# First modulation by column quarters beside the first four GLU units, later modulation in half-height blocks

## What is computed

```python
def modulation(c, w_ada, b_ada):
    m = jax.nn.silu(c) @ w_ada + b_ada              # 9 conditioning vectors; w_ada is 2048 x 12288
    return jnp.split(m[:, None, :], 6, axis=-1)

sh1, sc1, g1, sh2, sc2, g2 = modulation(c, w_ada, b_ada)
h = rmsnorm(x, norm1_g) * (1 + sc1) + sh1
z = h @ w_in                                        # 2048 x 5120
za, zg, q, k, v = jnp.split(z, ...)
u = za * jax.nn.sigmoid(zg)                         # the GLU, 1024 channels
```

## Time and profile before

| | us |
|---|---|
| runs | 3962.62, 3974.74, 3953.63 |
| span of the profiled execution (its own time is not listed apart from these) | 3945.3 |
| TensorE busy | 3630.9 |
| VectorE busy | 2664.1 |
| ScalarE busy | 446.6 |
| GpSimd busy | 1088.6 |

### The profile page before, as it was taken

One profiled execution on the slowest core, in us unless ns is written; L12 is line 12 of the kernel. 1 busy time (PEld: TensorE's weight loads), 2 busy tenths in 40 slices (PEclk: granted clock), 3 DMA queues, 4 the chain that ended last, 5 costly groups with the idle time before them and its releaser, 6 DMA issues.

```text
span 3945.3 us, 34389 instructions
## 1 busy us (share of the span) xinstructions
PE 3630.9 (92%) x12423; PEld 1928.8 (49%) x12423; DVE 2664.1 (68%) x4415; ACT 446.6 (11%) x975; POOL 1088.6 (28%) x865
## 2 busy tenths in 40 slices
PE   4899998997996799789989999999989899999997
PEld 1566544466552574356833444444455344444443
DVE  1258852148888885878976766677688765555666
ACT  2100004110000350011700000000043000000000
POOL 1000001106434543444153222222234422222331
PEclk8999999998998779899999999999999999999998
DMA  9878763459999998999699999999978999999997
GB/s 364 278 233 265 246 214 124 150 195 393 410 413 417 370 379 326 396 386 398 228 415 421 421 414 418 421 418 416 421 285 337 420 420 396 421 422 421 422 418 311
DMA packets 348738, 1402.89 MB, mean 356 GB/s; under 512 B 25601, under 2 KB 150489, under 8 KB 207606
## 3 DMA queue, kind: packets, MB, share of 16 engines
q0 software_dynamic: 117056, 832.57, 52.4%
q1 hardware_dynamic: 230512, 563.29, 38.1%
q10 hardware_dynamic: 1008, 4.98, 0.3%
HBM read 1375.24 MB, written 31.55 MB: 357 GB/s over the span
## 4 chain that ended last, share of the span: by engine, by line
DMA 48%; PE 27%; issue 14%; DVE 8%; POOL 3%; ACT 0%; SPq 0%; DVEq 0%; POOLq 0%; ACTq 0%
DMA R<-in_u_experts,MS 34%; DMA R<-in_v_experts,MS 10%; PE bank L868 8%; PE bank L896 7%; PE bank L1083 4%; DMA R<-in_w_ada 3%; POOL R L749 3%; DVE R L2242 2%; PE bank L808 1%; DVE R L2127 1%; DVE R L2034 1%; PE bank L785 1%; PE bank L1090 1%; DMA R<-h_scratch 1%; PE bank L1145 1%
## 5 line engine op out<-in xcount | busy, mean ns | idle before, releaser
L749 POOL DMA_INDIRECT R<-in_u_experts,MS x640 | 899.9, 1406 | 1639.2 <-DVE MS L2127 1354.6
L2127 DVE CUSTOM_DVE_ANT_0 R<-R 128x2048 f32<-128x2048 f32 x374 | 857.2, 2292 | 412.0 <-DMA R<-in_u_experts,MS 390.7
L1290 PE MATMUL bank<-R,RB 128*128 128x512 f32 x2304 | 1019.4, 600 | 46.9 <-DMA R<-in_v_experts 46.7
L1290 PE MATMUL bank<-RB 128*128 128x512 f32 x1792 | 778.2, 592 | 0.0
L1290 PEld LDWEIGHTS bank<-R,RB 128*128 128x128 f32 x2304 | 440.7, 192 | 615.5 <-issue 552.9
L2127 DVE CUSTOM_DVE_ANT_0 R<-R,RB 128x2048 f32<-128x2048 f32 x266 | 608.5, 2288 | 107.1 <-DMA R<-in_u_experts,MS 105.7
L1290 PEld LDWEIGHTS bank<-RB 128*128 128x128 f32 x1792 | 340.5, 190 | 428.6 <-issue 428.6
L2242 DVE SCALAR_TENSOR_TENSOR R<-R,MS 128x2048 f32<-128x2048 f32 x128 | 301.4, 2355 | 197.3 <-DMA R<-in_v_experts,MS 196.9
L868 PE MATMUL bank<-RB,R 128*128 128x256 f32 (+1 forms) x1536 | 400.4, 422 | 27.6 <-DMA R<-in_w_pq 24.4
L868 PEld LDWEIGHTS bank<-RB,R 128*128 128x128 f32 x1536 | 294.5, 193 | 126.4 <-DMA R<-in_w_pq 25.0
L1083 PE MATMUL bank<-RB,R 128*128 128x384 f32 x1024 | 333.3, 486 | 1.4 <-ACT RB L1450 0.7
(11 more groups left out here) (353 smaller groups left out, 2214.4 us busy)
## 6 DMA issues: line engine op xcount, KB each, us to landing
R<-in_v_experts SPq DMA_DIRECT2D x144, 1024.0 KB, 9.1
RB<-in_v_experts SPq DMA_DIRECT2D x112, 1024.0 KB, 9.3
R<-in_w_ada SPq DMA_DIRECT2D x48, 2048.0 KB, 13.2
R<-in_w_in SPq DMA_DIRECT2D x20, 2048.0 KB, 18.0
R<-in_w_in SPq DMA_DIRECT2D x24, 1024.0 KB, 28.4
R<-in_w_out SPq DMA_DIRECT2D x8, 2048.0 KB, 8.2
R<-in_w_pq SPq DMA_DIRECT2D x8, 2048.0 KB, 10.1
R<-in_w_out SPq DMA_DIRECT2D x16, 1024.0 KB, 15.9
```

Of the source, the lines that this page charges most:

```text
L749: pool.indirect_dma_start(dst, None, table, bass.IndirectOffsetOnAxis(ap=expert[T_ % 2][:, c:c + 1], axis=0)).then_inc(signal, 16)
L1290: x = pe.matmul(PB[4 * h + q][:, :], W[:, i, h * P:(h + 1) * P], vring[slot][:, q * PW:(q + 1) * PW], start=(i == 0), stop=(i == NKEY - 1))
L2127: V.tensor_tensor_reduce(u, u, x, 1.0, 0.0, ALU.mult, ALU.add, dots[t % 2][:, h * TOPK + s:h * TOPK + s + 1]).then_inc(dots_done, 1)
```

## The change

**First modulation in quarters.** The 4096 columns are cut into 32 pieces of 4 k by 512 columns, 1 MB each (`ada_piece`, four slots, in the place of ring slots 2 and 3). Order: column quarter q (0 to 3), in it scale, then shift, in it four groups of k. In a sum, the four k of a piece go to the four strips of rows (`ada_sums`), so that four pieces give 128 rows with the partial sums of 4 x 4 k. ACT copies them out (`keep_sums`), and `turn_mods` multiplies them with a 0/1 matrix (`group_sum`) onto the turned bias: this adds the four strips and turns them at once. Quarter q gives scale and shift for k = 4q to 4q+3. Sums of quarter 0 stand ahead of the projection (pieces 0 to 3 ahead of the transposes of x, 4 to 7 behind them and the conv cache), those of quarters 1 to 3 between the matmuls of the first four GLU units, which now run side by side over k in banks 0 to 5 (`first_unit`). With k = 12 to 15 the four units are finished one after another.

**Later modulation in halves.** 16 blocks of 512 columns, each in two halves of 8 k (`wide` slots 2 and 3, `modulate_half`, `load_ada_half`), 3, 3, 2 halves ahead of units 5, 6, 7 and so on (twelve units). None stands beside the first four units. DVE adds 16 blocks of 512 columns; its order of sums, convolutions and gates is written out.

**Start.** SP issues x first, then pieces 0 to 3, both w_in slots, and the other pieces. POOL makes its constants ahead of its loads, and issues the conv cache without a wait. DVE computes the distance rows first, ACT stores them. Two of the five squares of x move from ACT to DVE.

The core of the diff (semaphore counts that only follow are left out):

```diff
-            for n in range(NM1):
-                chunk, i = (1, n) if n < 8 else (0, n - 8)
...
+            for t in range(T):
+                sp.dma_start(xt[t], xp[t] if t < TP else xs).then_inc(s_x, 16)
+
+            def load_ada_piece(n):
+                q, shift, j = n // 8, n // 4 % 2, n % 4
+                if n >= 4:
+                    sp.wait_ge(mod_done, n - 3)
+                at = (0 if shift else D) + q * PW
+                sp.dma_start(ada_piece[:, j], wv["w_ada"][:, 4 * j:4 * j + 4, at:at + PW]).then_inc(s_bx[j], 16)
+
+            def load_ada_half(m):
+                c, half = divmod(m, 2)
+                sp.wait_ge(mod_done, ADA - 2 + 2 * m if m < 2 else ADA + m - 1)
+                sp.dma_start(wide[:, 2 + half], wv["w_ada"][:, 8 * half:8 * half + 8, 2 * D + c * PW:2 * D + (c + 1) * PW]
+                             ).then_inc(w_in_s[2 + half], 16)
+
+            for n in range(4):
+                load_ada_piece(n)
+            for b in range(2):
+                load("w_in", b, b * CC)
+            for n in range(4, ADA):
+                load_ada_piece(n)
+            for m in range(2):
+                load_ada_half(m)
+            for b in range(2):
+                sp.wait_ge(z_done, 2 * b + 2)
+                load("w_in", b, BW + b * CC)
+
+            m = 2
+            for u in range(12):
+                for _ in range(HALVES[u % 3]):
+                    if m < 2 * NMC:
+                        load_ada_half(m)
+                    m += 1
+                i, b, c = 1 + u // 4, u // 2 % 2, u % 2
+                if c == 1 and i < 3:
+                    sp.wait_ge(z_done, 4 + u + 1)
+                    load("w_in", b, (i + 1) * BW + b * CC)
...
+            def ada_sums(n):
+                q, shift, j = n // 8, n // 4 % 2, n % 4
...
+                for i in range(4):
+                    m = pe.matmul(PB[6 + shift][32 * i:32 * i + 32, :], cT32[:, 4 * j + i, :], ada_piece[:, j, i, :],
+                                  start=(j == 0), stop=(j == 3))
+                m.then_inc(mod_done, 1)
+
+            def turn_mods(q):
+                pe.wait_ge(s_mc, 2 * q + 2)
+                for shift in range(2):
+                    for i in range(4):
+                        at = (0 if shift else D) + (4 * q + i) * P
+                        out = PB[7][:, 64 * shift + 16 * i:64 * shift + 16 * i + NCND]
+                        pe.matmul(out, mrow[:, at:at + P], ident[32:32 + NCND, 32:32 + NCND],
+                                  start=True, stop=False)
+                        m = pe.matmul(out, mod_sums[shift][:, i * P:(i + 1) * P], group_sum, start=False, stop=True)
+                m.then_inc(s_modT, 1)
+
+            def modulate_half(m):
+                c, half = divmod(m, 2)
+                bank = PB[4 + (c + 2) % 4]
+                if half == 0 and c >= 4:
+                    pe.wait_ge(mod_free, c - 3)
+                elif half == 0 and c >= 2:
+                    pe.wait_ge(z_free, 3 + c)
+                pe.wait_ge(w_in_s[2 + half], 16 * (c + 1))
+                for k in range(8):
...
+                mm.then_inc(mod_done, 1)
...
+            for n in range(4):
+                ada_sums(n)
+            turn_x(0, KT + 4)
+            turn_conv_cache()
+            for n in range(4, 8):
+                ada_sums(n)
+            pe.wait_ge(s_bada, 32)
+            turn_mods(0)
             pe.wait_ge(cc_E, 4)
-            def glu_and_modulation(i, first):
...
+            for q in range(3):
+                n = 8 * (q + 1)
+                for i in range(4):
+                    for u in range(4):
+                        first_unit(u, 4 * q + i)
+                        if 4 * i + u in (0, 1, 3, 4, 6, 7, 9, 10):
+                            ada_sums(n)
+                            n += 1
+                        elif 4 * i + u == 12:
+                            turn_mods(q + 1)
+            for u in range(4):
+                for k in range(12, KT):
+                    first_unit(u, k)
+
+            m = 0
+            for u in range(12):
+                for _ in range(HALVES[u % 3]):
+                    modulate_half(m)
+                    m += 1
+                i, b, c = 1 + u // 4, u // 2 % 2, u % 2
+                pe.wait_ge(w_in_s[b], 16 * (i + 1))
+                pe.wait_ge(z_free, 4 + u + 1)
+                project((hTX, hTY), ring[:, b, :, c * P:(c + 1) * P], c, z_done)
...
+            for i, sums in enumerate((((0,), (1, 2), (3,), (4,)), ((5, 6), (7,), (8,), (9, 10)), ((11,), (12,), (13, 14), (15,)))):
+                for step in range(4):
+                    for c in sums[step]:
+                        modulated(c)
+                    if step < 2:
+                        conv(2 * i + step)
+                    else:
+                        gated(2 * i + step)
```

More of the change, by code:

```diff
@@ L371, in load @@
                 sp.dma_start(ring[:, j], wv[name][:, :, bass.ds(col, BW)]).then_inc(w_in_s[j], 16)
-            for n in range(NM1):
-                chunk, i = (1, n) if n < 8 else (0, n - 8)
-                if n >= NRING:
-                    sp.wait_ge(mod_done, n - 3)
-                sp.dma_start(tall[:, n % 4], wv["w_ada"][:, 2 * i:2 * i + 2, chunk * D:(chunk + 1) * D]).then_inc(w_in_s[n % 4], 16)
-            for j in range(2):
-                sp.wait_ge(mod_done, NM1 - 4 + j + 1)
-                load("w_in", j, j * CC)
@@ L382, in _ @@
-            for j in range(2):
-                sp.wait_ge(mod_done, NM1 - 2 + j + 1)
-                load("w_ada", 2 + j, (NM1 + j) * BW)
-            def beside(i, b, more):
-                w = i * 2 + b
-                for a in range(2, 6 if more else 4):
-                    sp.wait_ge(mod_done, w * 4 + (NM1 + a - 1))
-                    load("w_ada", 2 + a % 2, w * (4 * BW) + (NM1 + a) * BW)
-            with sp.Fori(0, 3) as i:
-                for b in range(2):
-                    beside(i, b, True)
-                    sp.wait_ge(z_done, i * 4 + (2 * b + 2))
-                    load("w_in", b, i * BW + (BW + b * CC))
@@ L404, in _ @@
             x_cols = [(4, 2, 3)[m // 4] * CC + (m // 2 % 2) * PW for m in range(12)]
+            sp.wait_ge(z_done, 14)
             load_x_half(0, "w_in", 0, x_cols[0])
-            beside(3, 1, False)
             sp.wait_ge(z_done, 16)
@@ L800, in _ @@
             t.then_inc(s_setT, 1)
[L802 to L816 removed]
+            pe.wait_ge(s_setE, 7)
@@ new lines, in modulate_half @@
+            def modulate_half(m):
[7 more added lines that the diff above has]
+                for k in range(8):
+                    g = k % 4
+                    mm = pe.matmul(bank[32 * g:32 * g + NCND, :], cT[:, 8 * half + k, :], wide[:, 2 + half, k, :],
+                                   start=(half == 0 and k < 4), stop=(half == 1 and k >= 4))
+                mm.then_inc(mod_done, 1)
@@ L1308, in _ @@
             act.wait_ge(s_x, 16 * T)
-            for t in range(T):
+            for t in range(3):
                 if t >= 1:
@@ L1727, in _ @@
                 TS(xt[t], xt[t], rs[:, t:t + 1], None, ALU.mult).then_inc(s_xn, 1)
-            for m in range(4, 8):
-                first_block(m)
             for c2 in range(4):
```

276 lines of the change are left out of this document (129 added, 147 removed).

## The result

The changed kernel takes 4053.03 us (median of 4 runs, 4041.59 to 4066.04); the kernel before, beside it on the same chip, 3958.12 (4 runs, 3949.92 to 3974.74). The ratio is 1.0239, 95% interval 1.0204 to 1.0275: slower, by 95 us. The forecast had +52 and a range that ended at +83. The profiled execution took 4048.32 us around a span of 4046.5, against 3945.3 before, +101.2; what follows accounts for these 101.2 us.

What follows compares the result with a forecast made beforehand. TensorE, busy 92% of the span, was taken as the bound, so E's delay reaches the total: 167 + 266.5 + 64 + 17 = 514.5 against 462, 52 us later, 4015 us; range 3977 to 4046.

Steps and rivals of the forecast that it cites:

- (a): Later modulation: 32 halves at 1.79 us each, 57.3 us in all before and after, at most 3.5 us more.
- (b): Front, until the first four units are done: first unit at 62.5, end at 167, net some 28 us saved.
- t0: Moment the first four units are done: forecast 167, bounds 150 and 182; far above 182 would show (b) wrong.
- the seams: Places in the front's quarters where the array tile's shape changes: eight per quarter at 0.25 us, bounds 0 and 0.98.
- (c): Twelve units behind the front: 12 x 17.43 us plus 57.3 us of halves, 266.5 us.
- (d): Third-half load waits ahead of eight of the twelve units: 5 x 6.4 + 3 x 10.6, 64 us; bounds 47 and 71.
- (e): TensorE's lower clock behind the eight waits: 2.1 us each, 17 us; bounds 0 and 22.
- E: Moment the sixteenth GLU unit ends, 462.05 us before; forecast 52 us later, the shift reaching the total undiminished.
- (f): Hidden work: DVE keeps up, TensorE never waits on its sums, later w_in loads start as before; no cost.
- The first (the third half costs little): Rival at the eight waits: something hides them, E 28 us early, 3934 us, faster; 7%.
- The third (front led by DMA, or dear seams): Rival: t0 at 182, waits 71, clock 22, E 83 us late, 4046 us; 17%.
- The second and fourth: Rivals: front better with waits at their least, 15 us late, 3977, 14%; DVE late with its sums, 2%.

Runs made afterwards that it cites:

- experiment 4: Changed kernel with b_ada left out of the first modulation, and with it one of the two matmuls per block of a turning: 4025.48 us, one run.
- experiment 5: Changed kernel with b_ada added by VectorE to the saved sums, each turning having 8 matmuls (16 records) in place of 16 (32 records): 4015.36 us, one run.
- experiment 9: Changed kernel with third half inside the unit, bias by VectorE, GpSimd's spread moved, b_ada's large part behind the first turning: 3938.85 us, 0.998 of the kernel before.
- experiment 7: Changed kernel with three edits: third half inside the unit, bias by VectorE, b_ada after x: 3950.70 us, ratio to the kernel before 0.9995.
- Experiment 1: Changed kernel with the third half of every triple summed inside the unit behind it, not ahead of it: 3971.96 us, ratio to the kernel before 1.0046.
- Experiment 8: Changed kernel with GpSimd's modulation save and bias-table spread moved behind the second value tile: 4035.16 us, one run.
- experiment 2: Changed kernel with each later w_in load issued behind the next half's load instead of ahead of it: 4044.63 us, one run.
- experiment 6: Changed kernel with both loads of b_ada issued only once x has landed, VectorE's wait for them moved too: 4063.6 us, one run.
- experiment 10: Kernel before with only the later modulation in halves, two behind each of the sixteen units, front unchanged: 3966.93 us, one run.

## Why the prediction was wrong

The direction and the main mechanism were right, the size wrong: +52 forecast, +95 measured, outside the range. By the steps:

**(a) Size of the halves: right.** 16 records take 1.78 to 1.88 us at full clock (1.79 taken), and the old kernel with halves alone moves nothing.

**(b) The front: wrong by 38.4 us** (205.4 in place of 167, beyond the bound of 182). This is the step that failed, in three of its terms, and t0 far above 182 is the sign that the prediction had named for it.
- *The turning*, "sixteen small fp32 matmuls, 2 us taken, 1.2 to 4 as bounds": it took 8.4 us the first time, then 5.1, 6.7 and 6.2, 26.4 in all where 8 were taken. The time was read off from transposes, which leave one record each. Here an fp32 matmul leaves two: the sixteen of a turning are 32 records. The text ahead of the forecast says so itself, has two blocks of 16 matmuls as x64, and step (e) and the first paragraph call records matmuls too (the 32 of the earlier trace rows, the 224 of L896). At the transposes' 2.06 us for 16 records, 32 would be 4.1; at full clock they took 5.1, and what the last 1.0 comes from, the change between two kinds of record perhaps, isn't shown. Experiments 4 and 5 show what hangs on the turnings: with half the records a later turning takes 1.85 us, the clock stays at 1.00, and from the first unit to t0 it is 105.8 and 105.4 us. The forecast for that was 87 + 17.4 = 104.4. So the seams, taken at 0.25 us each, weren't the trouble.
- *The clock behind the turnings* stood in step (e) for the later waits only. Here the three quarters, from 81.1 to 188.0, came to 106.9 us in place of 87, and the last part to 17.4 as forecast. Of these 19.9 us 12 are the three turnings themselves (18.0 less 6), and most of the rest the steps behind them at 0.50 (6.5 by experiment 5).
- *The first unit's start*, 81.1 in place of 62.5. The forecast started the transposes at 40, with the activations ready. But they stand behind the first four sums in TensorE's own order, and these waited for pieces landed at 37.4 and later, and ran at half speed: 47.8, 7.8 us late. The sums of pieces 4 to 7, taken at 0.95 each with the loads level, took 8.8 and not 4: 4.8 us. The turning gives 6.4, and the copies around it took 0.4 less than forecast: 18.6 together, of which up to 3.5 are the scatter of this moment. Under the first two lies the hole in the DMA rate, which the forecast left out by dividing the bytes by 0.39 MB/us: at that rate the 12 us would have moved 2.6 MB more, 6.7 us' worth. The earlier trace rows had the hint, 288 KB in 17.1 us; I used that line for when b_ada lands, and not for what it does to the loads beside it. In experiment 9, where b_ada's longer rows stand out of their way, the rate is 307 GB/s in that stretch, the first sum of w_ada starts 5.0 us earlier and the first unit 4.7 us earlier than in experiment 7, with b_ada just behind x. Even there t0 is 175.8, so 8.8 us of the front's miss are under neither edit.

The Trainium skill, page "DMA: Bandwidth & Descriptors", section "Queues, rings and completion order", says that each DMA engine takes turns between its queues and changes only when a packet of one queue is finished. A load of 1 MB on SP's queue is delayed by b_ada's long rows on GpSimd's: 23.8 to 26.1 us to landing with them beside it, 17.8 to 18.5 without. The rule would allow that; whether it is the reason no run here shows.

**(c) The twelve units: right**, 17.42 to 17.44 us each where no wait is ahead.

**(d) The eight waits: right**, 64.3 against 64, and in its parts: 13.6 us go when w_in no longer stands ahead (3 x (10.6 - 6.4) = 12.6 forecast). Experiment 1 takes nearly all of it away by one half's place. The chain shows 7.87 to 8.00 us from the first half's end to the landing in the plain cases, near the 8.2 of the earlier trace rows. The prediction's estimate of 6.8 us from the Trainium skill, page "DMA: Bandwidth & Descriptors", section "Anatomy of one DMA — SWDGE (gpsimd) path", would have given 53; that fit is for transfers that GpSimd issues, and these are SyncE's.

**(e) The clock behind the waits: right in the sum.** From t0 to E (205.41 to 552.47) it is 347.1 us, and less 266.5 and 64.3 that leaves 16.3, against 17. By the chain the eight third halves took 3.19 to 3.60 us each in place of 1.79, 13.6 us more together, and the twelve units 212.2 against 209.2, 3.0 more.

**(f) What is hidden: half right.** VectorE stays off the path: TensorE waits for it nowhere between t0 and E. But "everything behind E merely shifts" failed by 8 us, and the span moved by 101.2 where E moved by 90.3: that the sums of the modulation would be complete 14 us ahead of E and no longer 25 us behind it, and that GpSimd's transfers hang on this, was not worked out. Experiment 8 shows the cause.

**The rivals.** The first (the third half costs little) didn't occur, but experiment 1 builds it: it then comes to 3971.96 and not to 3934, since the front is 38 us worse than thought and w_in's wait is added. The third (front led by DMA, or dear seams) had the right place and, for half of it, the right mechanism: the start is led by the DMA, and the rest is the turnings and not the seams; its size, 182, was too small. That its total, 4046, comes near the measured one is in part luck, since it took waits and clock at 93 us where they were 80.6. The second and fourth didn't occur.

In one sum: the front saved 210 - 205.4 = 4.6 us and not 43, against 14.3 us of sums moved behind it, so it loses 9.7 where 28.7 were to be gained; the eight waits and their clock cost 64.3 + 16.3 = 80.6; the collision behind E costs 8.4. That is the 98.7 us by which the channel sums start late.

## What to carry to other kernels

When a load's start is tied to the use of the piece two before it, count the work between that use and the load's own: two pieces in a row with cover is a different program from three in a row, and here one half of each triple moved into the middle of its unit was worth 76 us. Count the records of the very kind of matmul that is added, not of a transpose of the same shape, and look at the clock that small matmuls leave behind. When an engine comes free earlier relative to its neighbours, the transfers that it releases start in a new place, and the load there may be one that somebody waits for.

## What the runs showed of the hardware

- The granted clock fell in a run of small matmuls though TensorE was shown busy throughout. With TensorE busy 5.00 of every 5.00 us, the stretch at the end of the second turning (110 to 115) has 0.67 and that of the third (145 to 150) 0.50; spread over four steps, 0.55 and 0.50 for 10 us. With 16 records of one kind in place of 32 of two, the clock stays at 1.00 through all three later turnings of experiments 4 and 5. The first turning comes behind waits: in experiment 9 its 16 records took 3.59 us, at 0.50.
- 432 KB in rows of 16 and 32 KB (nine rows each) pull all loads down while the DMA engines count as busy: 172 GB/s in the changed kernel (195 to 206 in six others with the same loads) and 237 before in the 12 us around them, 103 GB/s at a busy share of 0.79 in the 6 us to which they were moved, and 307 and 355 GB/s in the two stretches of 12 us from 16 to 40 where the longer rows were taken out.
- The score stage, which none of the edits touches, has two lengths: 47.8 to 49 us in eight of the twelve profiled executions, 61.3 to 61.6 in the others (experiments 2, 6, 7 and 10). The granted clock goes with it: the first line is of the kernel before, the second of experiment 7.

```profile
653.00:703.00 50.00, 37.24 (x172) 24.83 (x173) 19.66 (x117) 29.32 (x93) 12.17 (x22) 0.86 0.51 171
```
```profile
653.00:703.00 50.00, 47.22 (x139) 29.83 (x140) 15.54 (x94) 24.12 (x78) 8.03 (x14) 0.51 0.45 149
```

It comes and goes between kernels with the same code there, and it is as large as most of the differences looked for. It seems to make part of the spread of 20 to 38 us between runs of one kernel. In experiment 7 the profiled run, with 61.4 us in that stage, took 3963.89 us at a mean clock of 0.954; two others of the twelve are like it (3964.90 and 3967.12, at 0.953 and 0.954), and nine lie at 3946.59 to 3952.50, at 0.958 to 0.960. Only profiled runs show the stage itself, so this isn't shown for the others, and why the stage takes the one length or the other stays open. A single total of this kernel can't be read closer than that.
